# The attention's output projection in two parts by heads, the first four heads' part among the last head's steps

## The reference, cut to what matters

```python
q = _rms((xm @ w_q).reshape(B, T, A_HEADS, 2, A_DH), q_g) * (A_DH ** -0.5)
s = jnp.einsum('bqhcd,bkhcd->bhcqk', qblk, k_all)
p = jax.nn.softmax(jnp.where(mask, s + bias, NEG_BIG), axis=-1)
a = p[:, :, 0] - lam * p[:, :, 1]
o = jnp.einsum('bhqk,bkhe->bqhe', a, v_all)
...
o = _rms(o, head_g) * (1 - lam_init)
y = o.reshape(B, T, D_MODEL) @ w_o
...
x = x + g1[:, None, :] * y
xm = _modulate(x, p['norm_g'][l, 1], sh2, sc2)
x = x + g2[:, None, :] * _swiglu(xm, ...)
```

## Time and profile before

| What | Value |
| --- | --- |
| Time, median of 3 runs | 1569.48 us (1565.12 to 1569.79) |
| Profiled execution: its own time, span | 1569.69 us, 1567.9 us |
| Busy: PE, VectorE, ACT, POOL | 1510.9, 842.2, 416.5, 748.9 us |
| Chain that ended last | PE 89%, VectorE 5%, ACT 3%, issue 2% |
| Granted clock over the span | 0.98 of full |

### The profile page before, as it was taken

How to read it: one execution, slowest core, us unless ns; L and a number is a source line. 1 busy time by engine, 2 the same in 40 slices (tenths; PEclk the granted TensorE clock), 3 DMA queues, 4 the chain that set the end, 5 groups by cost and what they waited for, 6 DMA issues and landing times.

```text
span 1567.9 us, 31755 instructions
## 1 busy us (share of the span) xinstructions
PE 1510.9 (96%) x12494; PEld 1424.1 (91%) x12494; DVE 842.2 (54%) x1499; ACT 416.5 (27%) x894; POOL 748.9 (48%) x456
## 2 busy tenths in 40 slices
PE   5999999999999999999999989988899999999998
PEld 4998898999999999999997867767899999999998
DVE  6503455454342134445573167765557579557587
ACT  4302454221110011112211146665321123111132
POOL 2445333455454455554444423443455556455554
PEclk8999999999999999999999989977999999999999
DMA  9455413433536234343322332220122222222222
GB/s 363 129 174 166 133 68 109 153 131 122 197 142 235 88 122 187 134 166 128 99 71 67 95 135 83 83 76 21 54 81 80 82 89 88 91 81 80 85 93 98
DMA packets 53928, 183.49 MB, mean 117 GB/s; under 512 B 6232, under 2 KB 8672, under 8 KB 53584
## 3 DMA queue, kind: packets, MB, share of 16 engines
q1 hardware_dynamic: 51136, 174.63, 33.1%
q10 hardware_dynamic: 2704, 7.64, 1.3%
HBM read 171.69 MB, written 10.55 MB: 116 GB/s over the span
## 4 chain that ended last, share of the span: by engine, by line
PE 89%; DVE 5%; ACT 3%; issue 2%; DMA 0%; ACTq 0%; POOL 0%; SPq 0%; DVEq 0%; POOLq 0%
PE psum L656 61%; PE psum L702 7%; PE psum L898 7%; PE psum L667 3%; PE psum L1067 2%; PE psum L904 1%; PE psum L1120 1%; PE psum L1016 1%; PE psum L1107 1%; PE psum L997 1%; PE psum L805 1%; PE psum L1080 1%; PE psum L1150 1%; PE psum L834 1%; PE psum L1135 1%
## 5 line engine op out<-in xcount | busy, mean ns | idle before, releaser
L557 POOL TENSOR_SCALAR w_hi<-raw 128x1024 fp32r<-128x1024 f32 (+1 forms) x168 | 189.9, 1130 | 618.2 <-PE psum L656 495.0
L656 PE MATMUL psum<-act_hi,w_hi 128*128 128x288 f32 (+1 forms) x2048 | 448.2, 300 | 5.9 <-POOL w_lo L559 3.0
L656 PE MATMUL psum<-act_lo,w_hi 128*128 128x288 f32 (+1 forms) x2048 | 442.1, 297 | 0.0
L656 PE MATMUL psum<-act_hi,w_lo 128*128 128x288 f32 (+1 forms) x2048 | 442.0, 297 | 0.0
L559 POOL TENSOR_TENSOR w_lo<-raw,w_hi 128x1024 fp32r<-128x1024 f32 (+1 forms) x168 | 433.5, 2581 | 14.0
L656 PEld LDWEIGHTS psum<-act_hi,w_hi 128*128 128x128 f32 x2048 | 332.2, 190 | 12.0 <-issue 9.0
L656 PEld LDWEIGHTS psum<-act_hi,w_lo 128*128 128x128 f32 x2048 | 332.4, 190 | 0.0
L656 PEld LDWEIGHTS psum<-act_lo,w_hi 128*128 128x128 f32 x2048 | 331.9, 190 | 0.0
L656 PE MATMUL psum<-hid_both,w_hi 128*128 128x288 f32 x704 | 122.7, 297 | 0.0
L656 PEld LDWEIGHTS psum<-hid_both,w_hi 128*128 128x128 f32 x704 | 103.6, 189 | 0.6 <-issue 0.6
L1725 DVE SCALAR_TENSOR_TENSOR x<-psum,mod,x 128x288 f32 (+2 forms) x96 | 34.2, 412 | 99.9 <-PE psum L656 98.7
(11 more groups left out here) (320 smaller groups left out, 2222.3 us busy)
## 6 DMA issues: line engine op xcount, KB each, us to landing
raw<-in_w_stream SPq DMA_DIRECT2D x153, 512.0 KB, 3.5
ada_quad<-in_ada_w SPq DMA_DIRECT2D x48, 512.0 KB, 5.2
raw<-in_w_down SPq DMA_DIRECT2D x32, 704.0 KB, 4.2
ada_ring<-in_ada_w SPq DMA_DIRECT2D x32, 512.0 KB, 4.4
ada_first<-in_ada_w SPq DMA_DIRECT2D x8, 1024.0 KB, 15.7
line_rep<-line SPq DMA_DIRECT2D x8, 352.0 KB, 4.5
line<-line_rep SPq DMA_DIRECT2D x8, 352.0 KB, 5.3
x<-in_x SPq DMA_DIRECT2D x4, 576.0 KB, 5.8
```

The source lines that it names most:

```text
L557: pool.tensor_scalar(hi, src, 1.0, 0.0, ALU.mult, ALU.add).then_inc(hi_split, 1)
L656: last = mm(psum[:, b + half, 0:n_cols], weights[wp][:, k, :], parts[ap][:, k, half * HT:half * HT + n_cols], start=(k == 0 and n == 0), s ...
```

## The change

The output projection is made in units of another shape. `load_out(n)` fetches, in one transfer of the same 512 KB, half of two units: for n = 0 to 3 the k tiles of heads 0 to 3 of output tiles 2n and 2n+1, for n = 4 to 7 those of heads 4 to 7. `out_part(f)` is 12 matmuls, one output tile's half of the tokens over four heads; f = 0 to 15. The first twelve all go to PSUM bank 7, and VectorE adds each to x (`part_to_x`); the last four stay in banks 0 to 3. `out_rest(q)` is the other four heads for two output tiles, 48 matmuls, the last one on top of what stands in banks 0 to 3. Parts 0 to 7 lie in steps 1 to 4 of the last head, 8 to 10 beside its last turnings, 11 ahead of its sums, 12 to 15 behind. In heads 6 and 7 the sums of squares stand behind turning and values, and ACT reads them behind the exponential. GpSimd splits unit U_AO+2 within the last head.

```diff
@@ sync: loads
             for h in range(1, H):
-                load_unit(U_AQ + 2 + h)
+                load_unit(U_AQ + 2 + h) if h < H - 2 else load_out(h - (H - 2))
                 load_head(h)
-            load_unit(U_AO + 2)
-            load_unit(U_AO + 3)
-            load_pairs(U_AO + 4, 2)
+            for n in range(2, 8):
+                load_out(n)
@@ gpsimd: splits
+                if h == H - 1:
+                    split_unit(U_AO + 2)
                 if h >= 1:
...
-            split_pairs(119, 3)
+            split_unit(U_AO + 3)
+            split_pairs(U_AO + 4, 2)
@@ tensor
+            def out_part(f):
+                n, c = divmod(f, 4)
+                u, j, half = U_AO + n, c // 2, c % 2
+                pe.wait_ge(lo_split, u + 1)
+                if f == 0:
...
+                elif n < 3:
+                    pe.wait_ge(o_half_read, f)
+                elif c == 0:
+                    pe.wait_ge(scored, 5 * H)
+                for k in range(4):
+                    for i, (wp, ap) in enumerate(SPLIT3):
+                        last = mm(psum[:, 7 if n < 3 else c, 0:HT], w_parts[u % 2][wp][:, 4 * j + k, :],
+                                  act[BUF[A_O]][ap][:, k, half * HT:(half + 1) * HT],
+                                  start=(k == 0 and i == 0), stop=(n < 3 and k == 3 and i == 2))
...
+            def out_rest(q):
...
+                if q == 0:
+                    pe.wait_ge(o_half_read, 12)
...
+                else:
+                    for j in range(2):
+                        if q < 3:
+                            pe.wait_ge(o_x, 2 * q + j - 1)
+                        for k in range(4):
+                            k_tile(j, k)
...
+                if p == H - 1 and s >= 1:
+                    out_part(next(parts))
-                if s == 1 and p + 1 < H:
+                if s == 1 and not late:
                     query_sums(p + 1)
...
+                if s == 1 and p == H - 2:
+                    query_sums(p + 1)
+                    query_sums_sample(p + 1, late=True)
+                elif s == 3 and late:
+                    att_sums(p - 1)
+                    att_sums_sample(p - 1, late=True)
+                if (p == H - 1 and s >= 1) or p >= H:
+                    out_part(next(parts))
+            out_part(next(parts))
+            att_sums(H - 1)
+            att_sums_sample(H - 1)
+            for f in parts:
+                out_part(f)
+            for q in range(4):
+                out_rest(q)
@@ vector
+            def out_residual():
+                def pair(i, banks=4):
+                    for j in range(2):
...
+                        last.then_inc(o_x, 1)
+                        ve.wait_ge(o_x, i * 2 + (j + 1))
+                        if banks == 0:
+                            ve.sem_inc(evac[j], 4)
+                        scaled_lo(A_FFN1, gain_of(3), j, i)
+                        acc_tile(N_FFN1, j, i)
+                loop(ve, 3, pair)
+                pair(3, 0)
...
+                if g > 5 * H - 4:
+                    part_to_x(2 * (g - (5 * H - 4)) - 1)
                 if g >= 1:
                     att_weight(g - 1)
+                if 5 * H - 4 <= g < 5 * H:
+                    part_to_x(2 * (g - (5 * H - 4)))
```

More of the change, by code:

```diff
@@ L1135, in att_sums, with att_sums_sample @@
                 mm(psum[:, 6, :], mean_sq, tmp[:, 0, 0:TP], start=True, stop=True)
[L1137 removed]
+            def att_sums_sample(h, late=False):
                 pe.wait_ge(o_out, h + 1)
[L1140 removed]
+                pe.wait_ge(at_ready, min(5 * H, 5 * h + 6 + late))
                 mm(psum[:, 4, 448:512], mean_sq, tmp[:, 0, TP:T], start=True, stop=True).then_inc(oms_ready, 1)
[L1143 to L1148, removed]
[L1149 to L1154 removed]
+            def out_part(f):
[3 more added lines that the diff above has]
+                if f == 0:
+                    pe.wait_ge(evac[(U_AQ + 7) % 2], (U_AQ + 7) // 2 + 1)
+                    pe.wait_ge(lo_ready[A_O], 4)
+                elif n < 3:
[7 more added lines that the diff above has]
+                                  start=(k == 0 and i == 0), stop=(n < 3 and k == 3 and i == 2))
+                if c == 3:
+                    last.then_inc(unit_done, 1)
+                else:
+                    last.then_inc(o_half_mm, 1)
@@ new lines, in out_rest, with k_tile @@
+            def out_rest(q):
+                u = U_AO + 4 + q
+                pe.wait_ge(lo_split, u + 1)
+                bank = lambda j: 4 + 2 * j if q < 3 else 2 * j
+                def k_tile(j, k):
+                    for i, (wp, ap) in enumerate(SPLIT3):
+                        for half in range(2):
+                            last = mm(psum[:, bank(j) + half, 0:HT], w_parts[u % 2][wp][:, 4 * j + k, :],
+                                      act[BUF[A_O]][ap][:, 4 + k, half * HT:(half + 1) * HT],
+                                      start=(q < 3 and k == 0 and i == 0), stop=(k == 3 and i == 2))
+                    if k == 3:
+                        last.then_inc(unit_done if j else o_done, 1)
+                if q == 0:
+                    pe.wait_ge(o_half_read, 12)
+                    pe.wait_ge(o_out, H)
+                    pe.wait_ge(oz_ready, H)
+                    for k in range(4):
+                        pe.wait_ge(lo_ready[A_O], 5 + k)
+                        for j in range(2):
+                            k_tile(j, k)
+                else:
+                    for j in range(2):
+                        if q < 3:
+                            pe.wait_ge(o_x, 2 * q + j - 1)
+                        for k in range(4):
+                            k_tile(j, k)
@@ L1156, in _ @@
             pe.wait_ge(v_tail, 4)
+            parts = iter(range(16))
             for g in range(5 * H + 3):
                 p, s = divmod(g, 5)
+                late = p >= H - 2
                 if g == 0:
@@ L1579, in _ @@
                     att_by_key(g - 2)
-                if s == 1 and queries:
+                late = p >= H - 2
+                if s == 1 and queries and not late:
                     query_z(p + 1)
@@ L1583, in _ @@
                     out_sample(p - 1)
-                elif s == 3 and out:
+                elif s == 3 and out and not late:
                     z_sample(p - 1)
@@ L1588, in _ @@
                 att_exp(g)
+                if s == 1 and queries and late:
+                    query_z(p + 1)
+                elif s == 3 and late:
+                    z_sample(p - 1)
                 if s == 0 and p >= 1 and queries:
@@ L2148, in _ @@
                     head_lo(5)
+            for f in range(8, 11):
+                part_to_x(f)
             head_lo(H - 2)
+            part_to_x(11)
             z, y, t, o = (tmp[:, n, :] for n in (1, 2, 3, 5))
```

66 lines of the change are left out of this document (41 added, 25 removed).

## The result

| | Before | After |
| --- | --- | --- |
| Median of 4 runs | 1568.61 us (1565.12 to 1569.79) | 1584.8 us (1582.43 to 1590.72) |
| Ratio | 1 | 1.0113 [1.0079, 1.0146] |
| Profiled execution, span | 1569.69, 1567.9 us | 1583.57, 1581.4 us |

What follows compares the result with a forecast made beforehand. PE was taken as the late engine, through 12.2 us of waits and its halved clock. Stages -9.8 + 12.9 + 3.1 - 7.7 = -1.5, clock +6.4, gave +4.9: 1574.5 us, range 1563 to 1583.

Steps and rivals of the forecast that it cites:

- the clock: Attention's last two heads: one low stretch of 15.9 us, PE busy for 0.8 at half speed, +6.4 us.
- the residual stage: First residual to norm sums: VectorE's chain of eight tiles sets the length, 42.2 us instead of 49.9, -7.7.
- Head 6: Head 6's stage: late sums of squares remove PE's 2.7 us wait, clock stays up; 17.3 us instead of 27.1, -9.8.
- Last head: Last head's steps: moved matmuls 12.8 us, bank waits 6.0, starting wait for VectorE 4.8; 36.5 us, +12.9.
- either rival's: Both heads: clock stays 1.00, 1568 us, chance 0.24; or low stretch lasts 27 us or more, 1580.5, chance 0.23.
- Tail: From the last head's steps to the first residual: 23.6 us, +3.1, including 0.6 for the bank.
- 7 x 4.57: Residual stage: seven tile intervals of VectorE's chain at 4.57 us each, with splits beside four of eight tiles.
- the upper bound of 4.90: Residual stage: 4.90 us for every tile, with a first FFN unit wholly at half speed, gives -1.6.
- the 9.05 charged: End of the residual stage: 6.45 us in the sum after the tiles, plus 2.6 for PE's half-speed start.
- The fast rival: Last head: VectorE reads odd parts before the score, so the 6.0 us of bank waits vanish; 1561 us, chance 0.15.
- The rival without effect of the late sums: Head 6: late sums shorten no wait, gaining nothing beyond the clock; within the 1580.5 rival's range, no chance of its own.

Runs made afterwards that it cites:

- short splits: Both mends, plus GpSimd's subtraction of six weight splits beside the residual stage done over 16 of 1024 columns; ratio to the kernel before 0.9982.
- both mends: Changed kernel with VectorE's odd-part read ahead of the last head's scores, and the banks of output tiles 6 and 7 exchanged; ratio to the kernel before 1.0011.

## Why the prediction was wrong

The direction and the places held; the size didn't: 1574.5 forecast, 1584.8 measured, and 1.8 above the range. Two terms of the sum were too small, the clock and the residual stage. The parts of the sum, one by one, from the two profiled executions:

- **Head 6.** Late sums win, as forecast; the late sums alone show it on their own (19.6). Of the 2.3 us over the forecast, 1.7 are half of the 3.4 us at the lower level with PE fully busy, which belong to the clock, 0.6 is the stage.
- **Last head.** The waits were forecast at 6.0 for the bank and 4.8 at the start, and were 7.1 (1.99, 3.41, 1.69) and 3.6 (2.0 for the weighting, 1.6 for the low part): 10.7 for 10.8. The hit is partly luck, since the 3.41 holds 1.16 of the moved split, which I had named with up to 2.4 us and not added. PE's busy time was 33.3 where the work at full speed is 25.7, so the clock took 7.6.
- **Clock.** The failed step, first half: "I take their mean, 15.9 us, once". It was not once but five stretches, 20.5 us in all, from 1050.9 to 1098.6, each beside one of the waits of 1.7 to 3.4 us that the change left or made. It cost 1.7 + 7.6 = 9.3 instead of 6.4. The low time was nearer the forecast than either rival's, neither none nor 27 us; but PE was busy for 0.9 of it and not for the 0.8 that I took.
- **Tail.** 24.5 for 23.6. The bank wait of 0.7 was forecast as 0.6; the rest is PE's own work, 23.8 for 23.0. The last head's chain and the first late splits are covered, as forecast.
- **Residual stage.** The failed step, second half: "7 x 4.57". The mechanism held: VectorE's chain bounds it, PE stands (6.2 us, forecast 7 to 10), the FFN starts at half speed. But the tiles are 35.07 / 7 = 5.01 us apart, above even the upper bound of 4.90. Those without a split took 4.14 (I had read 4.23), those with one 4.99 to 6.60, since their low parts took 1.78 to 3.39 where I had 1.61. The earlier trace rows showed one such meeting, in which the low part began 2.7 us after its split, with 0.9 of the subtraction left. In the changed kernel three of four met a subtraction with 1.6 us or more still left, and the third tile's met the scaling before it as well; the fourth of them, 1.78, met only the scaling. That is 3.1 us. The FFN unit took 8.5 of the 9.05 charged, which gives 0.5 back. The kernel with short splits shows what the subtractions cost with both mends: 5.5 us.

Together: 0.6 - 0.1 + 2.9 + 0.9 + 2.6 = 6.9, the difference of the sums 132.9 and 126.0. The forecast's other shortfall is not in these stages: 1.4 us ahead of head 6, 0.3 behind the norm sums. From +4.9 to the +13.5 of the spans that leaves nothing. The medians lie 16.2 apart: the profiled execution of the changed kernel was 1.2 under its median, that of before 1.1 above. So how far the median lies above the range is in part chance: the 1.4 ahead of head 6, which the change doesn't touch, is most of the 1.8.

By the Trainium skill, "SBUF — State Buffer", section "Who interferes with whom", the one of the two that is issued second blocks wholly. By that rule the 4.57 was the wrong sum, since it took the length of the wait from one meeting, whereas a whole block lasts as long as what is left of the split. The trace agrees: the second instruction of the low part of 1138.52 began 0.4 us after the subtraction and ended at 1141.91, the subtraction at 1141.82.

The fast rival named the right place: with the read ahead of the score 1.0036, and with both mends 1.0011. It doesn't win, and the stages of both mends and of the late sums alone show where. The residual stage of the first has 145 matmuls fewer, which is 19.4 us at 0.1335 each (an estimate), but it is only 9.5 us shorter (40.4 for 49.9), since VectorE sets its length; last head and tail, where these matmuls went, are 14.6 us longer (60.7 for 46.1). The rival without effect of the late sums is refuted. What stays open is why a wait is followed by a short low stretch here, by a long one there and by none elsewhere: after 1.99 us it lasted 6.8 in the changed kernel, and 17.1 in the kernel with the late sums alone; after the 2.48 for the last low part there was none at once in the kernel before, and one of 3.4 us in the late sums alone.

## What to carry to other kernels

Before matmuls are moved into a stage, look at who reads their PSUM bank and what stands ahead of that read in the reader's queue: a score in front of it cost 0.77% here. When PE's time per tile is halved, add up the other engine's chain per tile, and price each meeting of VectorE with a GpSimd instruction by what is left of that instruction, not by one example. Count both instructions of a split. Where PE must wait for short times anyway, dense unneeded matmuls in the gap may pay: the late sums alone gave 0.34%, with filler in the heads 0.43%, with the tail filled too 0.57%. These steps are within the noise of the timing, but the sums of the stages go the same way (115.6, 112.5, 109.6). The moved real work, which brought its own waits, lost 1.3%.

## What the runs showed of the hardware

The granted clock fell to its lower level beside waits of 2.0 us (ended at 1050.75, 1060.16 and 1074.47 in the changed kernel, 1060.62 in the late sums alone) and one of 1.7 (1095.04), where the profile before had led me to look at 2.7 and more. Once low it stayed low for 17.1 us with PE busy for 16.1 of them. With 72 matmuls that nobody reads in the same two heads it was 1.00 throughout, though there the waits in these heads were shorter as well, 0.9 us at most.

VectorE's two-instruction low part took 0.95 us where it met neither instruction of a GpSimd split, 1.73 and 1.78 where it met only the scaling, and 1.61 to 3.97 beside a subtraction. A VectorE instruction on 128x2 elements took 1.33 beside one instead of 0.17, and ended 0.02 us after it.
